# Moving the triangular systems and decayed query-key products of a gated DeltaNet layer from the chunk stream into the projection phase, through DRAM

## What is computed

```python
def chunk_gated_delta(q, k, v, g, beta):
    gc = jnp.cumsum(g, axis=-1)
    decay = jnp.exp(jnp.where(incl, gc[..., :, None] - gc[..., None, :], -jnp.inf))
    kb = k * beta[..., None]
    a_mat = jnp.where(strict, jnp.einsum("bhnid,bhnjd->bhnij", kb, k) * decay, 0.0)
    ...
    sol = lax.linalg.triangular_solve(a_mat + eye, rhs, left_side=True, lower=True, unit_diagonal=True)
    u, w = sol[..., :dv], sol[..., dv:]
    qk = jnp.einsum("bhnid,bhnjd->bhnij", q, k) * decay
    ...
    def step(s, inp):
        v_new = u_n - w_n @ s
        o = qd_n @ s + qk_n @ v_new
        s = s * gt_n + kt_n.T @ v_new
```

## Time and profile before

| | us |
|---|---|
| median of 3 runs (lowest, highest) | 3242.26 (3238.85, 3243.62) |
| the profiled execution, device time | 3243.82 |
| its span, first to last instruction | 3242.1 |
| PE, ACT, DVE, POOL busy in it | 2779.4, 1224.1, 1628.7, 1253.5 |
| dn_project, first to last unit on PE | 1135.9 to 1760.8 |
| dn_chunks, first matmul to last period's end | 1783.2 to 2903.8 |
| mean granted clock of PE | 0.926 |

### The profile page before, as it was taken

How to read it: one execution, slowest core, us unless ns; L and a number is a source line. 1 busy time by engine, 2 the same in 40 slices (tenths; PEclk the granted TensorE clock), 3 DMA queues, 4 the chain that set the end, 5 groups by cost and what they waited for, 6 DMA issues and landing times. The chain is left out here.

```text
span 3242.1 us, 53074 instructions
## 1 busy us (share of the span) xinstructions
PE 2779.4 (86%) x19211; PEld 2661.3 (82%) x19211; DVE 1628.7 (50%) x2351; ACT 1224.1 (38%) x1989; POOL 1253.5 (39%) x1183
## 2 busy tenths in 40 slices
PE   4799999993997299999997998999989999995993
PEld 2788888883995199999996898888989889885992
DVE  3266666664202334444443776776767677663003
ACT  2255555553103134334433344534444453432001
POOL 3333333331220122222221766665666666642220
PEclk8899999996998599999998999998999899997996
DMA  3111111112314023332232312032131313114214
GB/s 108 53 52 52 52 52 52 52 39 87 111 65 171 19 72 90 94 93 88 85 91 69 92 18 74 17 78 51 40 77 17 74 17 76 28 17 145 79 39 170
DMA packets 187727, 223.34 MB, mean 69 GB/s; under 512 B 50715, under 2 KB 157548, under 8 KB 185884
## 3 DMA queue, kind: packets, MB, share of 16 engines
q1 hardware_dynamic: 182940, 203.98, 21.7%
q10 hardware_dynamic: 4608, 17.04, 1.6%
HBM read 152.77 MB, written 68.23 MB: 68 GB/s over the span
## 5 line engine op out<-in xcount | busy, mean ns | idle before, releaser
L1634 ACT ACTIVATE zz<-ps 104x416 fp32r<-104x416 f32 x560 | 284.9, 517 | 446.4 <-PE ps L1496 445.3
L537 PE MATMUL ps<-dn_yhi,dn_whi 128*128 128x416 f32 (+1 forms) x1152 | 387.1, 336 | 16.4 <-POOL dn_wlo L521 16.4
L538 PE MATMUL ps<-dn_ylo,dn_whi 128*128 128x416 f32 (+1 forms) x1152 | 376.1, 326 | 0.0
L539 PE MATMUL ps<-dn_yhi,dn_wlo 128*128 128x416 f32 (+1 forms) x1152 | 375.1, 326 | 0.0
L1726 DVE TENSOR_TENSOR pp<-ps,level_mask 104x416 fp32r<-104x416 f32 x560 | 318.8, 586 | 100.1 <-PE ps L1496 97.7
L1498 PE MATMUL ps<-pp,zz 104*104 104x208 f32 x1440 | 266.1, 295 | 41.4 <-ACT zz L1634 31.9
L537 PE MATMUL ps<-rg_yhi,rg_whi 128*128 128x416 f32 (+1 forms) x768 | 251.9, 328 | 45.8 <-POOL rg_wlo L521 40.4
L538 PE MATMUL ps<-rg_ylo,rg_whi 128*128 128x416 f32 (+1 forms) x768 | 251.6, 328 | 0.0
L539 PE MATMUL ps<-rg_yhi,rg_wlo 128*128 128x416 f32 (+1 forms) x768 | 250.6, 326 | 0.0
L1498 PE MATMUL ps<-zz,pp 104*104 104x208 f32 x1440 | 247.9, 282 | 0.0
L1498 PEld LDWEIGHTS ps<-pp,zz 104*104 104x104 f32 x1440 | 184.4, 176 | 67.2 <-ACT zz L1634 34.8
(11 more groups left out here) (275 smaller groups left out, 7476.8 us busy)
## 6 DMA issues: line engine op xcount, KB each, us to landing
dn_raw<-in_dn_w_in SPq DMA_DIRECT2D x48, 512.0 KB, 3.9
qd<-rows_scratch SPq DMA_DIRECT2D x160, 104.0 KB, 3.1
rg_raw<-in_rg_w_in SPq DMA_DIRECT2D x32, 512.0 KB, 3.8
o_scratch<-a SPq DMA_DIRECT2D x16, 520.0 KB, 2.8
rgo_oraw<-o_scratch ACTq DMA_DIRECT2D x16, 520.0 KB, 4.3
n_y<-y_scratch SPq DMA_DIRECT2D x16, 520.0 KB, 6.5
n_h<-h_scratch SPq DMA_DIRECT2D x16, 520.0 KB, 12.6
qk_scratch<-p_qk SPq DMA_DIRECT2D x16, 520.0 KB, 3.1
```

What stands on the lines that cost most here:

```text
L537: e.matmul(o, whi, mhi[:, t0:t0 + tn], start=(first and k == 0), stop=False)
L538: e.matmul(o, whi, mlo[:, t0:t0 + tn], start=False, stop=False)
L539: ins = e.matmul(o, wlo, mhi[:, t0:t0 + tn], start=False, stop=(last and k == end))
L1634: e.activation(zz[:, b, :, :], ps[0:CH, 2 * b + 1, 0:m4], ACT.Copy).then_inc(zev.sem, 1)
```

## The change

- `dn_tables` also stores the running sums of the decay rates as rows (`rows_dram[1]`) and keeps them as columns (`gc`).
- `dn_project` makes for each head and each of its 10 chunks, once for both directions: the product of keys with keys and queries (PE `products`, one matmul of 104x208, and ACT `products_out`, a copy to `raw`), the decays (SP `load_decays`, four loads that spread the rows over 104 partitions; POOL `differences`, four instructions of 104x104 a chunk; ACT `decays`, one Exp), the masked products with decay (DVE `systems`, three instructions of 104x416 a chunk), times beta (POOL `strengths`, two of 104x208), and stores them (SP `store_nq`, 338 KB a chunk). Tiles for them lie partly in `sq` and `rn`, so both sums of squares and both norms move ahead, beside unit 3, and keys are turned in unit 4, values in unit 5 through banks 0 to 2.
- `dn_chunks` loses `pre` on PE, ACT and DVE, and on POOL all but the two with the identity; SP loads the stored matrices, up to ten steps ahead (`load_systems`, two of 169 KB a step).
- `final` is spread over two periods: five Ln of 128x416 in one, five Exp, scalings and gatings in the next. The next head's loads and the store are issued a period later (p = 8).

The core of the diff:

```diff
@@ dn_project, SP @@
+            def load_decays(n):
+                e.wait_ge(nb_done.sem, nb_done.at(n, 0))
+                e.wait_ge(qkt_done.sem, qkt_done.at(n, 0))
+                for d in range(2):
+                    for r in range(2):
+                        src = gc_rows[d][bass.ds(n * 2 + r, 1), :].rearrange("r (k i) -> (r k) i", i=CH)
+                        e.dma_start(ex[:, :, d, r, :], src.partition_broadcast(CH)).then_inc(ex_in.sem, 16)
...
             def turn(n, last):
+                load_decays(n)
                 load(n, 4), load(n, 5)
                 ahead(0)
                 store_qk(n, 0)
                 ahead(1)
                 store_qk(n, 1)
+                store_rows(n, krow_dram, krow.rearrange("c k m -> c (k m)").unsqueeze(1), 3, krow_out)
+                store_nq(n, 0, 1)
                 ahead(2)
-                store_rows(n, krow_dram, krow.rearrange("c k m -> c (k m)").unsqueeze(1), 3, krow_out)
+                store_nq(n, 2)
                 store_z(n, 0)
+                store_nq(n, 3, 4, 5)
+                ahead(3)
                 store_rows(n, vrow_dram, vrow.rearrange("c k r m -> c (k r m)").unsqueeze(1), 8, vrow_out)
-                ahead(3)
+                store_nq(n, 6, 7, 8, 9)
                 store_z(n, 1)
@@ dn_project, POOL @@
-                for j in range(6):
-                    wt.split_unit(e, n, j, tile, j - 1)
+                split(n, 2)
+                differences(0, 1, 2, 3, 4)
+                split(n, 3)
+                differences(5, 6, 7, 8, 9)
+                split(n, 4), split(n, 5)
+                strengths(0, 1, 2, 3)
+                if not last:
+                    split(n + 1, 0)
+                strengths(4, 5, 6, 7, 8, 9)
+                if not last:
+                    split(n + 1, 1)
@@ dn_project, PE @@
+            def values_by_tokens(n, q):
+                if q == 0:
+                    e.wait_ge(z_out.sem, z_out.at(n, 2))
+                    e.wait_ge(silu.sem, silu.at(n, 4))
...
+            def products(n, k):
+                if k < 2:
+                    e.wait_ge(row_done.sem, row_done.at(n, k + 2))
+                    e.wait_ge(normed.sem, normed.at(n, 2))
                 else:
+                    e.wait_ge(raw_done.sem, raw_done.at(n, k - 1))
+                e.matmul(ps[0:CH, 7 - k % 2, 0:2 * CH], qk[:, 0, cs(k)], qk[:, :, cs(k)], start=True, stop=True) \
+                    .then_inc(gram.sem, 1)
...
+                e.wait_ge(row_done.sem, row_done.at(n, 0))
                 unit(n, 0)
                 e.wait_ge(z_out.sem, z_out.at(n, 0))
                 unit(n, 1)
@@ dn_project, ACT @@
+                copy_in(0), tanh(0), square(0), copy_in(1), tanh(1), square(1), copy_in(2)
                 inverse_norm(0)
-                copy_in(3), tanh(3)
                 inverse_norm(1)
+                keys_out(0), keys_out(1), keys_out(2)
+                decays(0, 1, 2, 3, 4)
+                copy_in(3)
+                decays(5, 6, 7, 8, 9)
+                products_out(0, 1)
+                tanh(2)
+                products_out(2, 3)
+                tanh(3)
                 z(0)
+                products_out(4, 5, 6, 7)
+                values_out(0)
...
@@ dn_project, DVE @@
+                        e.tensor_tensor(gm[:, b], raw[:, k].unsqueeze(1).to_broadcast([CH, 2, 2, CH]),
+                                        c["gram_mask"][:, :, :, :], ALU.mult).then_inc(gm_done.sem, 1)
+                        e.wait_ge(gm_done.sem, gm_done.at(n, k + 1))
...
+                        for q, done in enumerate((nb_done, qkt_done)):
+                            e.tensor_tensor(nq[k % RING][:, :, q],
+                                            gm[:, b, :, q, :].unsqueeze(2).to_broadcast([CH, 2, 2, CH]),
+                                            ex[:, k], ALU.mult).then_inc(done.sem, 1)
...
+                conv(0), silu_of(0), conv(1), silu_of(1), conv(2)
+                norm(0), norm(1)
+                systems(0)
+                conv(3)
+                systems(1)
+                silu_of(2)
+                systems(2)
+                silu_of(3)
+                z(0)
+                systems(3, 4, 5, 6, 7, 8, 9)
+                z(1)
@@ dn_chunks @@
+    LN_AT, EXP_AT, SCALE_AT, GATE_AT = [3, 4, 5, 6, 8], [3, 4, 5, 6, 8], [4, 5, 6, 7, 9], [5, 6, 7, 8, 9]
...
-                if p % PAIRS == 1 and p >= 6:
-                    final((p - 6) // PAIRS, l)
+                if p >= 6 and p % PAIRS in (1, 2):
+                    final((p - 6) // PAIRS, SLOTS * (p % PAIRS - 1) + l)
...
+            def load_systems(n, g):
+                if g >= NC:
+                    e.wait_ge(om.sem, om.at(n, g - NC + 1))
```

More of the change, by code:

```diff
@@ L1173, in inverse_norm, with decays @@
                                  bias=c["q_bias" if i else "k_bias"][:, 0:1]).then_inc(rn_done.sem, 1)
+                def decays(*chunks):
+                    for k in chunks:
+                        e.wait_ge(diff.sem, diff.at(n, k + 1))
+                        v = ex[:, k].rearrange("p d r i -> p (d r i)")
+                        e.activation(v, v, ACT.Exp).then_inc(e_done.sem, 1)
                 def z(i):
@@ L1205, in _ @@
+                products_out(9)
+                values_out(2), values_out(3), values_out(4)
                 z(1)
@@ L1386, in turn @@
             def turn(n, last):
-                for p in range(2, 2 * PAIRS + 2):
-                    if p == 2:
-                        load(n, 1)
-                    if p == 7:
+                for p in range(3, 2 * PAIRS + 3):
+                    if p == 8:
                         store(n, 0)
@@ L1393, in turn @@
                             load(n, 2)
-                    if not last or p < 2 * PAIRS:
-                        decay_rows(n, 2 * p), decay_rows(n, 2 * p + 1)
+                    for g in (2 * p + 4, 2 * p + 5):
+                        if not last or g < STEPS:
+                            load_systems(n, g)
+                    for g in (2 * p, 2 * p + 1):
+                        if not last or g < STEPS:
+                            decay_rows(n, g)
                 store(n, 1)
+                if not last:
+                    load(n, 3)
+            for g in (0, 1):
+                load_systems(0, g)
             load(0, 0)
-            for g in range(4):
+            for g in range(2, NC):
+                load_systems(0, g)
+            for g in range(6):
                 decay_rows(0, g)
+                if g == 1:
+                    load(0, 1)
             with e.Fori(0, TURNS - 1) as n:
```

461 lines of the change are left out of this document (238 added, 223 removed).

## The result

| | us |
|---|---|
| changed kernel, median of 4 runs (lowest, highest) | 3361.1 (3355.32, 3371.6) |
| kernel before, on the same chip, median of 4 runs | 3242.94 (3238.85, 3247.4) |
| ratio, 95% interval | 1.0369 [1.0342, 1.0395] |
| span of the profiled execution | 3355.3, clock 0.913 |

The account below looks back on a forecast made before the run. PE was taken to bound dn_project and dn_chunks. Terms: dn_tables +4, dn_chunks -173, dn_project +201, sum +32 on the profiled 3243.8, 3276; median forecast 3274 us, own range 3235 to 3330, eight in ten 3170 to 3340.

Parts of the forecast that it names:

- The loop through four queues: dn_project: late systems, POOL's split, SP's queue and POOL's differences delay unit 3, making a turn 104 us (95 to 112).
- 20 differences, 0.24 each: dn_project, POOL after the decays land: 20 differences at 0.24 us each, 4.8 us ahead of unit 3's split.
- 2 for the clock: dn_project, unit 3: PE returns from its wait at the lower clock, costing about 2 us a turn.
- a taking of turns: dn_project: DVE and POOL alternate whole instructions reading SBUF; seven systems, their strengths and a split's subtraction take 21.2 us.
- the upper bound of 0.45: dn_project, POOL: top of the range of 0.2 to 0.45 us given for one difference.
- the eight in ten: Whole kernel: the range expected to hold eight times in ten, from faster to slower rival, 3170 to 3340 us.
- Without them I count a wait of 0.2 us for pp: dn_chunks periods: PE loses 2.28 us of work but waits 0.2 for DVE's pp, so gains 2.1 a period.
- worth nothing: dn_chunks periods: fewer instructions on DVE, ACT and POOL gain nothing by themselves, as none of these was the bound.
- The finals: dn_chunks: spreading removes PE's 2.4 us wait and slow clock, leaving 0.7 of 11.5 us a final.
- The start of dn_chunks: Before the first inversions, one small load and one POOL instruction remain in front: -10 us (0 to -15).
- Decays in time: Rival, dn_project: POOL and DVE hardly meet, decays come faster, a turn takes 90 us, 3173 in all; chance 0.28.
- The rival of a stream that gains less: dn_chunks: 1 us less gained a period and 5 us left a final, 39 + 30, so 3343 us; chance 0.10.

Follow-up runs that it names:

- diffs_dve: Changed kernel, but DVE makes the 40 differences of a turn and POOL splits weights without them in between: 3200.8 us, ratio 0.9887.
- no_strengths: Changed kernel, but POOL's strengths multiply 2 columns of each matrix and not 104: 3342.4 us in one run.
- final_alone: Kernel before with only the final spread over two periods, next head's loads and store a period later: 3178.4 us, ratio 0.9813.
- all moved: Changed kernel with differences on DVE, decays loaded earlier, head's tables in slot 4, ACT's and DVE's dn_project work reordered: 3121.6 us, ratio 0.9635.

## Why the prediction was right in its mechanism and wrong in its size

**Right.** The loop through four queues sets the turn; the runs with the split first, the decays earlier and the differences on DVE each take it apart at another link, and the turn moves each time. In the changed kernel's turn (us after unit 3's start; forecast, measured): first product copied 29.2 and 29.5; z(0) done 44.4 and 43.5; systems with their strengths 65.5 and 62.3; split of the next unit 1 69.0 and 65.8; decays landed 94.0 and 91.4, so 25 and 25.6 for the way there.

**Wrong: the term "20 differences, 0.24 each".** They took 0.72 each, 14.4 us instead of 4.8, on top of a chain that was 2.6 shorter: 109.2, not 102.3 with 2 for the clock. Of the 14.4, some 12.2 are POOL's own (the second twenty of a turn take 12.2 to 12.9 behind the first turn); the rest comes beside DVE's conv, a taking of turns that the forecast counted at the systems and not here. That the chain was shorter is luck: a system with its strengths took 2.18 us and not 2.69, seven of them 3.6 less. The 2 us for the clock are there (17.0 us from unit 3 to unit 4, against 15.2 in diffs_dve), but they delay none of the chain's links and add nothing to it. The mean of the seven, with a first that was longer still, is 110.2: 7 x 6.2 = 43 of the 47 us.

I took a cast of the same shape for the price, since it was the nearest row in size. The other row, 0.60 us for a multiplication of 256 columns, was nearer in kind; the run with constants (0.56) shows that the operand isn't what makes a difference dear. By that row as it stands twenty take 12 us, seven turns 7 x 7.2 = 50 more, and the forecast is 3324; the upper bound of 0.45, had it been that 0.60, would have put the forecast's range at 3351 and the eight in ten at 3361, just at the measured time. But that the row fits is chance: a strength of 208 columns takes 0.53 us at the least here and one of 4 columns 0.2 (no_strengths), so by its size a multiplication of 104 would take some 0.36, an estimate, and twenty 7. No row of the kernel before has the price of this instruction, and that called for a wider bound.

**Wrong: "Without them I count a wait of 0.2 us for pp", and DVE's fewer instructions "worth nothing".** The step looked at the mean period and not at the one where a head begins. There DVE has the head's tables to copy and, since the final is spread, a scaling as well; PE waits 1.6 to 1.7 us, and in some heads 6 to 10 us at the lower clock follow. The run with later tables puts some 20 of the 36 us on that. The spread final was thought to leave 0.7 us a head and nothing at a head's start; final_alone has the wait of 1.7 us with the products still there. And the relief of DVE and POOL counted for something: moving the tables gains 22 us with it and loses 16 without it.

**Missing: the jump back.** The forecast has no term for the two jumps of the loop. In the run with later tables their periods are 10 us over their kind, in the run with all moved 5. In the kernel before PE stands still there too (3.08 and 2.66 us), but five periods with a final and a jump take 141.3 and 141.7 us, those with a final alone 140.2 to 142.0: the rows of before give the jump no price, and what hid it there is open.

**The finals**, forecast to leave 0.7 each: a head without the late waits takes 119.7, against (128.9 - 5 x 2.1) + 0.7 = 119.1. Apart from the wait at a head's start that step was right. The start of dn_chunks, forecast 10 us shorter, was not: 2 longer with the tail in front of it, since what came sooner (the inversions' second level began 36.8 us after the last unit before, and 31.1 now) was taken back by a first pair at the lower clock: 22.9 us from there to its end, not 14.9.

**The rivals.** Decays in time (3173) had them land at 80 and unit 3 split at 87; they landed at 91.4, and it was split at 109.2. Its turn of 90 came about another way, with the differences on DVE (88.6, 3201), which want the decays later and hold up no split. The rival of a stream that gains less had the right place, pp at a level with nothing in front, though in one slot of a head and not at all levels; 36 us against its 69.

The rule of the Trainium skill on how many engines a transfer uses ("DMA: Bandwidth & Descriptors", section "Why a DMA increments its semaphore by 16 and not by 1") would have added 3 us a turn to the way of the decays. It measured 25.6 where I had 25 without it, and no run here sets the two apart.

## What to carry to other kernels

Price an instruction by one of its own kind on its own engine, not by one of its shape, and where no row has one, give it a wide bound, above all where it stands ahead of something that every turn of a loop waits for: here forty small ones between POOL's splits make a turn of 109.7 us, and the same forty on DVE one of 88.6. When work is taken away or spread, look at the one period where the other engines have most to do, not at the mean one: a copy or a scaling ahead of the next operand costs more there than its own length, if the clock falls behind the wait. And when a change joins several edits, time them apart: half of this one's gain in dn_chunks came from the spread final, which needed none of the move and alone makes the kernel 1.9% faster.

## What the runs showed of the hardware

- A `TENSOR_SCALAR` of two operations on 104x104 takes 0.63 us on POOL and 0.19 on DVE (20 in 3.76 us).
- A plain copy on DVE is held up by POOL as well, for a whole instruction. In the changed kernel, beside a split's subtraction:

```profile
1682.49 0.17 DVE L1363 COPY p_gcol<-gc 104x40 f32 x1
1682.58 2.39 DVE L1364 COPY p_bcol<-beta 104x40 f32 x1
...
1682.49 2.44 POOL L523 TENSOR_TENSOR dn_wlo<-dn_raw,dn_whi 128x1024 fp32r<-128x1024 f32 x1
```

0.17 us for one copy, 2.39 for the next. My forecast had this only for instructions that read two operands in SBUF. The Trainium skill has it for copies too: in "SBUF — State Buffer", section "SBUF: two separate sides", a POOL instruction and a DVE operation in a two-port mode share a pair of ports, and whichever starts first holds it for its whole instruction; an fp32 copy within SBUF triggers such a mode. The trace agrees: the copy ends with POOL's instruction.
- A jump back to a loop's start stalls PE for 1.8 to 3.5 us at both jumps of dn_chunks, with no wait that the profile shows, in all kernels here. Its cause stays open; no run tried it.
- The same wait of 1.57 us in PE's stream, at the same place of a head, was followed by 6 us at the lower clock in one head of the changed kernel (start 2849.14, period 28.5) and by none in another (start 2230.37, period 25.5); one of 1.73 was followed by 10 us. What decides it stays open.
